# Differential attention beside slab matmuls: logits of two steps behind every second slab, their weights' transposes in the middle of a later one

## Chip, cores and metric

One core of one Trainium2 chip. The time is the device time of one launch in microseconds; several runs are taken and their median is compared.

## The reference

Two blocks of two layers each on 512 tokens of width 1024. The stage in question belongs to the first block (`first_block`), once in each of its two layers: four heads of differential attention, whose scores come in two maps of width 64.

```python
scores = jnp.einsum('bqhmd,bkhmd->bhmqk', qb, kh)
p = jax.nn.softmax(jnp.where(mask, scores, -jnp.inf), axis=-1)
w = p[:, :, 0] - lam * p[:, :, 1]
return jnp.einsum('bhqk,bkhd->bqhd', w, vf)
...
merged = (g[:, :, 0] * (y_a @ w_branch_a[layer])
          + g[:, :, 1] * (y_b @ w_branch_b[layer])
          + g[:, :, 2] * (y_c @ w_branch_c[layer]))
```

## The kernel before

**Slabs.** Every dense product runs as slabs of 128 x 1024 weights in three terms of fp32r (high x high, high x low, low x high; lines 576 to 578), 24 matmuls of 512 columns for a slab of eight tiles (`slab_t`, line 585). A slab is loaded by SP into one of four raw buffers as soon as the slab four before it is done (`load`, line 547), its high part made by ACT (`split_hi`, line 562, called as `hi_ahead` for the slab three on) and its low part by DVE in place (`split_lo`, called as `lo_ahead` for the slab three on, line 571). All engines run in program order, so a wait holds whatever stands behind it.

**The fill stage.** Attention of the first block is spread over 19 slabs (`FILLS1`, `for n in range(FILLS1)` on PE at line 2251, ACT at 1018, DVE at 1572): slabs 0 to 4 are gates of branch b, 5 to 12 branch b's product (`w_branch_b`), 13 to 18 gates of branch c. Sixteen steps (four heads h by four query tiles qi) go with them. Step n has logits for two maps of (qi + 1) x 128 columns, each map in 64 rows of the array (line 2276), so that the two run beside each other.

- PE: slab n with its `between(k)` ahead of tile k; behind the slab the logits of step n, then the transposes of the weights of step n - 2 (`LAG`), qi + 1 of them (line 657). `by_v` of head h (line 2231) stands ahead of tile 3 of slab 4h + 6 (`PV1_AT`) and first waits until the four steps' transposes have been copied out.
- DVE at step n: causal mask, maximum and its negative for both maps (lines 1580 to 1582); in slabs 0 to 3 two casts of `yb` to its high part (line 1588), whose low part POOL then makes (line 560); from slab 5 on the merge of branch b (lines 1595 and 1599); then, once both exponentials have left their banks, the weights of step n (lines 1606 to 1610); last `lo_ahead` of slab n.
- ACT at step n: `hi_ahead` of slab n; the copy of `by_v`'s result (line 1023); copies of gates (line 957); the copies of the transposed weights of step n - 2 (line 1048); the exponentials of step n (line 1057).

**PSUM.** `pm` has four banks, used in turn in the order in which the schedule `PM` hands out numbers: `take_pm` (line 639) makes PE wait until use i - 4 has been left (`pm_free`). Logits take two uses a step, transposes and `by_v` one each. The order of `PM.take` calls (lines 348 to 357) must be that of PE's program.

**Other buffers.** Exponentials and weights of step n lie in `ee[n % 3]`; the exponentials of step n wait for the transposes of step n - 3.

Of the kernel before, what the change touches and what calls it, by code (L numbers as in the profile page):

```python
# [10 lines left out]
ACT = mybir.ActivationFunctionType  # L11
# [102 lines left out]
def program(nc, t, out, depth=DEPTH, depth2=DEPTH):  # L114
    with ExitStack() as ctx:
# [231 lines left out]
        SUMS_AT = FILLS1 - 2  # L347
        for n in range(FILLS1):
            if n in PV1_AT:
                PM.take(("pv", PV1_AT.index(n)), 1)  # L350
            if n == SUMS_AT:
                PM.take("sub_first", 1)
            if n < STEPS:
                PM.take(("score", n), 2)
            if LAG <= n < STEPS + LAG:
                PM.take(("w_t", n - LAG), 1)
# [459 lines left out]
        def _(act):  # L816
# [48 lines left out]
            for l in range(depth):  # L865
# [152 lines left out]
                for n in range(FILLS1):  # L1018
# [8 lines left out]
                    if n == SUMS_AT:  # L1027
                        u = PM["sub_first"]
                        nc.scalar.activation(sub_sum[:, 0:DA_H - 1, :].rearrange("p h t -> p (h t)"), sums_of(pm_filled(act, u), TT * (DA_H - 1)), ACT.Copy)\
                            .then_inc(pm_free[u % 4], 1)  # L1030
                    if n < GATES_B_IN:
                        gates(gate, SL["gate_b"], UN["gate_b"], KD - GATES_B_IN + n, 1, ACT.Copy)
# [8 lines left out]
                    if LAG <= n < STEPS + LAG:  # L1041
                        k = n - LAG
                        h, qi, u = k // TT, k % TT, PM[("w_t", k)]
                        if h >= 2:
                            act.wait_ge(pm_ready, PM[("pv", h - 2)] + 1)
                        bank = pm_filled(act, u)
                        for kt in range(qi + 1):
                            done = nc.scalar.activation(wt(h, kt)[:, (qi - kt) * P:(qi - kt + 1) * P], bank[:, kt * P:(kt + 1) * P], ACT.Copy)
                        done.then_inc(pm_free[u % 4], 1)
                    if n < STEPS:  # L1050
                        qi = n % TT
                        if n >= 3:
                            act.wait_ge(pm_ready, PM[("w_t", n - 3)] + 1)
                        for m in range(2):
                            u, o = PM[("score", n)] + m, 8 * n + 2 * m
                            act.wait_ge(S("neg_max"), past("neg_max") + 2 * n + m + 1)
                            nc.scalar.activation(ee[n % 3][:, m, 0:(qi + 1) * P], pmb(u)[:, 0:(qi + 1) * P], ACT.Exp,
                                                 bias=sst[:, o + 1:o + 2], scale=DA_D ** -0.5,
                                                 accum_out=sst[:, 8 * n + 4 + m:8 * n + 5 + m]).then_inc(pm_free[u % 4], 1)
# [259 lines left out]
        def _(dve):  # L1319
# [44 lines left out]
            for l in range(depth):  # L1364
# [207 lines left out]
                for n in range(FILLS1):  # L1572

                    if n < STEPS:
                        qi = n % TT
# [1108 lines left out]
```

## Time and profile before

| | us |
|---|---|
| median of three runs | 2553.91 (2553.7 to 2556.19) |
| the profiled execution, its time | 2558.13 |
| the profiled execution, its span | 2556.4 |
| PE busy in the span | 2535.5 |
| DVE busy | 1598.4 |
| ACT busy | 1171.6 |
| POOL busy | 323.0 |

The fill stage of the first layer lies at about 364 to 500 us, that of the second at about 1290 to 1431. In the rows a matmul counts from its start; matmuls overlap, so the distance between two starts, not the duration, is what one costs. An fp32 product shows as two matmul instructions.

### The profile page before, as it was taken

Reading aid. Unit: us, or ns where it says so; the run is one execution under the profiler, and the core shown is the slowest. Engines: PE = TensorE matmul, PEld = TensorE weight load, DVE = VectorE, ACT = ScalarE, POOL = GpSimd, SP = SyncE. Lnnn points to the kernel's source line nnn. Section 1 sums busy time; section 2 is a strip of 40 time slices with the busy share of each in tenths; the row PEclk is TensorE's granted clock in tenths of the full one; section 3 lists DMA queues with packets and bytes.
Section 4 is the critical chain, followed back from the end, with each engine's and each line's share of the span. In section 5 each row is a group of like instructions: output and inputs, shape, how many; then the busy total and the mean of one; then the engine's idle time right before and its main releaser. Section 6 shows DMA issues by size and latency. Waiting matters only on the chain.

```text
span 2556.4 us, 34401 instructions
## 1 busy us (share of the span) xinstructions
PE 2535.5 (99%) x12345; PEld 2059.7 (81%) x12345; DVE 1598.4 (63%) x2484; ACT 1171.6 (46%) x2124; POOL 323.0 (13%) x256
## 2 busy tenths in 40 slices
PE   8999999999999999999999999999999999999998
PEld 7887887788888887887877888888888777887777
DVE  6745767567777336637667457775345677647765
ACT  6434544434433235436353444333246555575463
POOL 1024200010111001225010201110010001110010
PEclk9999999999999999999999999999999999999999
DMA  5543342333333455442443333333324322332322
GB/s 128 104 83 66 85 90 75 62 103 91 98 98 92 100 104 89 91 79 71 92 82 64 82 95 93 96 98 93 100 79 107 83 65 61 87 95 75 83 61 72
DMA packets 417919, 221.93 MB, mean 87 GB/s; under 512 B 52705, under 2 KB 400897, under 8 KB 417537
## 3 DMA queue, kind: packets, MB, share of 16 engines
q1 hardware_dynamic: 417792, 220.26, 35.5%
q8 instruction: 78, 1.28, 0.2%
q14 instruction: 49, 0.39, 0.1%
HBM read 218.12 MB, written 2.10 MB: 86 GB/s over the span
## 4 chain that ended last, share of the span: by engine, by line
PE 93%; DVE 2%; DMA 2%; ACT 1%; issue 1%; POOL 0%; SPq 0%; ACTq 0%; DVEq 0%
PE pg L576 28%; PE pg L578 27%; PE pg L577 27%; PE pm L657 3%; DMA w_raw<-in_w_in_dram 1%; PE pm L2395 1%; DVE w_lo L571 1%; PE pm L2276 1%; PE pm L2369 1%; PE pm L2231 1%; PE pm L2179 1%; PE pm L2409 1%; PE pm L2436 1%; ACT w_hi L566 0%; PE pm L2182 0%
## 5 line engine op out<-in xcount | busy, mean ns | idle before, releaser
L571 DVE TENSOR_TENSOR w_lo<-w_raw,w_hi 128x1024 fp32r<-128x1024 f32 (+3 forms) x440 | 535.4, 1218 | 485.0 <-ACT w_hi L566 482.9
L576 PE MATMUL pg<-h_hi,w_hi 128*128 128x512 f32 x1856 | 738.0, 398 | 1.1 <-DVE conv_in L1804 0.8
L566 ACT ACTIVATE w_hi<-w_raw 128x1024 fp32r<-128x1024 f32 (+3 forms) x440 | 434.7, 988 | 641.4 <-DMA w_raw<-in_w_in_dram 279.1
L578 PE MATMUL pg<-h_hi,w_lo 128*128 128x512 f32 x1856 | 723.9, 390 | 0.0
L577 PE MATMUL pg<-h_lo,w_hi 128*128 128x512 f32 x1856 | 723.5, 390 | 0.0
L576 PEld LDWEIGHTS pg<-h_hi,w_hi 128*128 128x128 f32 x1856 | 349.3, 188 | 74.6 <-issue 6.0
L578 PEld LDWEIGHTS pg<-h_hi,w_lo 128*128 128x128 f32 x1856 | 348.7, 188 | 74.2
L577 PEld LDWEIGHTS pg<-h_lo,w_hi 128*128 128x128 f32 x1856 | 349.3, 188 | 68.7 <-issue 1.0
L576 PE MATMUL pg<-w_hi,h_hi 128*128 128x512 f32 (+2 forms) x448 | 167.3, 373 | 0.6 <-issue 0.6
L578 PE MATMUL pg<-w_hi,h_lo 128*128 128x512 f32 (+2 forms) x448 | 165.1, 369 | 0.0
L577 PE MATMUL pg<-w_lo,h_hi 128*128 128x512 f32 (+2 forms) x448 | 165.0, 368 | 0.0
L1669 DVE SCALAR_TENSOR_TENSOR arena<-conv_in,par,arena 128x512 f32<-128x512 f32 x176 | 131.8, 749 | 15.2 <-DVE arena L1669 10.6
L576 PE MATMUL pg<-f_hi,w_hi 128*128 128x512 f32 x352 | 138.7, 394 | 0.0
L578 PE MATMUL pg<-f_hi,w_lo 128*128 128x512 f32 x352 | 138.0, 392 | 0.0
L577 PE MATMUL pg<-f_lo,w_hi 128*128 128x512 f32 x352 | 136.6, 388 | 0.0
L1105 ACT ACTIVATE arena<-conv_in,par 128x512 f32<-128x512 f32 x88 | 71.9, 817 | 114.3 <-DVE conv_in L1663 114.3
L560 POOL TENSOR_TENSOR f_lo<-arena,f_hi x44 | 56.8, 1291 | 519.8 <-DVE f_hi L1677 519.8
L1663 DVE TENSOR_TENSOR conv_in<-pg,rinv 128x512 f32<-128x512 f32 x88 | 60.8, 691 | 88.7 <-PE pg L578 79.7
L576 PE MATMUL pg<-nb_parts,w_hi 128*128 128x512 f32 x256 | 102.5, 401 | 0.0
L578 PE MATMUL pg<-nb_parts,w_lo 128*128 128x512 f32 x256 | 100.6, 393 | 0.0
L576 PEld LDWEIGHTS pg<-w_hi,h_hi 128*128 128x128 f32 x448 | 84.4, 188 | 13.9 <-issue 1.9
L578 PEld LDWEIGHTS pg<-w_hi,h_lo 128*128 128x128 f32 x448 | 84.3, 188 | 12.9
(405 smaller groups left out, 3765.2 us busy)
## 6 DMA issues: line engine op xcount, KB each, us to landing
w_raw<-in_w_in_dram SPq DMA_DIRECT2D x184, 512.0 KB, 5.0
w_raw<-in_ffn_w_up_dram SPq DMA_DIRECT2D x88, 512.0 KB, 3.8
w_raw<-in_w_out_dram SPq DMA_DIRECT2D x32, 512.0 KB, 3.9
w_raw<-in_ffn_w_down_dram SPq DMA_DIRECT2D x32, 512.0 KB, 3.8
w_raw<-in_w_branch_b_dram SPq DMA_DIRECT2D x16, 512.0 KB, 3.8
w_raw<-in_ffn_w_down_dram SPq DMA_DIRECT2D x16, 384.0 KB, 3.4
w_raw<-in_w_branch_a_dram SPq DMA_DIRECT2D x16, 256.0 KB, 2.8
w_raw<-in_w_branch_c_dram SPq DMA_DIRECT2D x16, 256.0 KB, 2.8
```

The costliest lines, as they stand in the source:

```text
L560: return nc.gpsimd.tensor_tensor(lo, value, hi.bitcast(F32), ALU.subtract)
L566: nc.scalar.activation(w_hi[:, s % HI, 0:n], w_raw[:, s % RAW, 0:n], ACT.Copy).then_inc(hi_done, 1)
L571: nc.vector.tensor_tensor(w_lo[:, s % RAW, 0:n], w_raw[:, s % RAW, 0:n], w_hi[:, s % HI, 0:n].bitcast(F32), ALU.subtract)\
L576: nc.tensor.matmul(dst, l_hi, r_hi, start=start, stop=False)
L577: nc.tensor.matmul(dst, l_hi, r_lo, start=False, stop=False)
L578: return nc.tensor.matmul(dst, l_lo, r_hi, start=False, stop=stop)
L657: done = nc.tensor.transpose(dst, src, ident[0:src.shape[0], 0:src.shape[0]])
L1105: nc.scalar.activation(facc[:, j, :], conv_in[:, j, 4:4 + SEQ], ACT.Identity, bias=fconv_b[:, bass.ds(i, 1)], scale=fconv_w[:, i, 2:3]).th ...
L1663: nc.vector.tensor_tensor(conv_in[:, j, 4:4 + SEQ], unit_filled(dve, SL["up"] + j, UN["up"] + j, 4, it), inv[:, :], ALU.mult)\
L1669: nc.vector.scalar_tensor_tensor(facc[:, j, :], conv_in[:, j, 4 - a:4 - a + SEQ], fconv_w[:, i, 2 - a:3 - a], facc[:, j, :], ALU.mult, ALU ...
L2179: done = nc.tensor.matmul(bank[rows, c * P:(c + 1) * P], xdt[:, c, h * 64:h * 64 + 64], seg[:, h % 4, c, :], start=True, stop=c == 0)
L2231: done = nc.tensor.matmul(bank[:, kt * P:SEQ], qkv[:, kt, 1024 + h * P:1024 + (h + 1) * P], wt(h, kt), start=kt == 0, stop=kt == TT - 1)
```

## The change

Logits of steps n and n + 1 follow each other behind slab n for even n (`SCORES_AT`), none behind odd slabs. The transposes of both steps stand together ahead of tile 4 of slab n + 2 (`W_AT`), no longer behind a slab. ACT and DVE take two steps at even n and none at odd n; ACT's copies of the transposed weights now stand ahead of the gates' copies. The numbers in `PM` follow the new order.

```diff
--- before.py
+++ after.py
@@ -345,15 +345,18 @@
         GATES_C_IN = FILLS1 - KD - GATES_B_IN
         PV1_AT = [TT * (h + 1) + LAG for h in range(DA_H)]
         SUMS_AT = FILLS1 - 2
+        SCORES_AT, W_AT = range(0, STEPS, 2), range(2, STEPS + 1, 2)
         for n in range(FILLS1):
             if n in PV1_AT:
                 PM.take(("pv", PV1_AT.index(n)), 1)
+            if n in W_AT:
+                PM.take(("w_t", n - 2), 1)
+                PM.take(("w_t", n - 1), 1)
             if n == SUMS_AT:
                 PM.take("sub_first", 1)
-            if n < STEPS:
+            if n in SCORES_AT:
                 PM.take(("score", n), 2)
-            if LAG <= n < STEPS + LAG:
-                PM.take(("w_t", n - LAG), 1)
+                PM.take(("score", n + 1), 2)
         PM.take("sub_last", 1)
         PM.take("sub_spread", DA_H)
         for name in ("sums2", "spread2"):
@@ -1028,6 +1031,14 @@
                         u = PM["sub_first"]
                         nc.scalar.activation(sub_sum[:, 0:DA_H - 1, :].rearrange("p h t -> p (h t)"), sums_of(pm_filled(act, u), TT * (DA_H - 1)), ACT.Copy)\
                             .then_inc(pm_free[u % 4], 1)
+                    for k in (n - 2, n - 1) if n in W_AT else ():
+                        h, qi, u = k // TT, k % TT, PM[("w_t", k)]
+                        if h >= 2:
+                            act.wait_ge(pm_ready, PM[("pv", h - 2)] + 1)
+                        bank = pm_filled(act, u)
+                        for kt in range(qi + 1):
+                            done = nc.scalar.activation(wt(h, kt)[:, (qi - kt) * P:(qi - kt + 1) * P], bank[:, kt * P:(kt + 1) * P], ACT.Copy)
+                        done.then_inc(pm_free[u % 4], 1)
                     if n < GATES_B_IN:
                         gates(gate, SL["gate_b"], UN["gate_b"], KD - GATES_B_IN + n, 1, ACT.Copy)
                     if n == GATES_B_IN:
@@ -1038,25 +1049,16 @@
                     if i >= 0:
                         act.wait_ge(S("b_merged"), past("b_merged") + i + 1)
                         gates(gate, SL["gate_c"], UN["gate_c"], i, 1, ACT.Copy)
-                    if LAG <= n < STEPS + LAG:
-                        k = n - LAG
-                        h, qi, u = k // TT, k % TT, PM[("w_t", k)]
-                        if h >= 2:
-                            act.wait_ge(pm_ready, PM[("pv", h - 2)] + 1)
-                        bank = pm_filled(act, u)
-                        for kt in range(qi + 1):
-                            done = nc.scalar.activation(wt(h, kt)[:, (qi - kt) * P:(qi - kt + 1) * P], bank[:, kt * P:(kt + 1) * P], ACT.Copy)
-                        done.then_inc(pm_free[u % 4], 1)
-                    if n < STEPS:
-                        qi = n % TT
-                        if n >= 3:
-                            act.wait_ge(pm_ready, PM[("w_t", n - 3)] + 1)
+                    for k in (n, n + 1) if n in SCORES_AT else ():
+                        qi = k % TT
+                        if k >= 3:
+                            act.wait_ge(pm_ready, PM[("w_t", k - 3)] + 1)
                         for m in range(2):
-                            u, o = PM[("score", n)] + m, 8 * n + 2 * m
-                            act.wait_ge(S("neg_max"), past("neg_max") + 2 * n + m + 1)
-                            nc.scalar.activation(ee[n % 3][:, m, 0:(qi + 1) * P], pmb(u)[:, 0:(qi + 1) * P], ACT.Exp,
+                            u, o = PM[("score", k)] + m, 8 * k + 2 * m
+                            act.wait_ge(S("neg_max"), past("neg_max") + 2 * k + m + 1)
+                            nc.scalar.activation(ee[k % 3][:, m, 0:(qi + 1) * P], pmb(u)[:, 0:(qi + 1) * P], ACT.Exp,
                                                  bias=sst[:, o + 1:o + 2], scale=DA_D ** -0.5,
-                                                 accum_out=sst[:, 8 * n + 4 + m:8 * n + 5 + m]).then_inc(pm_free[u % 4], 1)
+                                                 accum_out=sst[:, 8 * k + 4 + m:8 * k + 5 + m]).then_inc(pm_free[u % 4], 1)
 
                     if n == STEPS - 1:
                         act.wait_ge(slab_done, SL["b"] + KD)
@@ -1571,10 +1573,10 @@
                 chain(nc.vector.scalar_tensor_tensor(lstat[:, 4:5], lstat[:, 3:4], lam_c[:, 0:1], lstat[:, 2:3], ALU.subtract, ALU.subtract))
                 for n in range(FILLS1):
 
-                    if n < STEPS:
-                        qi = n % TT
+                    for k in (n, n + 1) if n in SCORES_AT else ():
+                        qi = k % TT
                         for m in range(2):
-                            u, o = PM[("score", n)] + m, 8 * n + 2 * m
+                            u, o = PM[("score", k)] + m, 8 * k + 2 * m
                             bank = pm_filled(dve, u)
                             diag = bank[:, qi * P:(qi + 1) * P]
                             chain(nc.vector.tensor_tensor(diag, diag, causal, ALU.add))
@@ -1598,14 +1600,14 @@
                         unit_left(dve, UN["a"] + i)
                         nc.vector.tensor_tensor(m_val[:, i, :], m_val[:, i, :], gate[:, i, :], ALU.add).then_inc(S("b_merged"), 1)
 
-                    if n < STEPS:
-                        w = (n % TT + 1) * P
+                    for k in (n, n + 1) if n in SCORES_AT else ():
+                        w = (k % TT + 1) * P
                         for m in range(2):
-                            pm_left(dve, PM[("score", n)] + m)
-                        o = 8 * n + 4
+                            pm_left(dve, PM[("score", k)] + m)
+                        o = 8 * k + 4
                         chain(nc.vector.reciprocal(sst[:, o + 2:o + 4], sst[:, o:o + 2]))
                         chain(nc.vector.tensor_scalar(sst[:, o + 3:o + 4], sst[:, o + 3:o + 4], lstat[:, 4:5], None, ALU.mult))
-                        e0, e1 = (ee[n % 3][:, m, 0:w] for m in range(2))
+                        e0, e1 = (ee[k % 3][:, m, 0:w] for m in range(2))
                         chain(nc.vector.tensor_scalar(e0, e0, sst[:, o + 2:o + 3], None, ALU.mult))
                         nc.vector.scalar_tensor_tensor(e0, e1, sst[:, o + 3:o + 4], e0, ALU.mult, ALU.add).then_inc(S("w_ready"), 1)
                     lo_ahead(FILL0() + n, 0, 0)
@@ -2258,6 +2260,11 @@
                             heads_t(k // 2)
                         if n in PV1_AT and k == 3:
                             by_v(PV1_AT.index(n))
+                        if n in W_AT and k == 4:
+                            for step in (n - 2, n - 1):
+                                pe.wait_ge(S("w_ready"), past("w_ready") + step + 1)
+                                transposes(pe, PM[("w_t", step)], lambda bank: [(bank[:, kt * P:(kt + 1) * P], ee[step % 3][:, 0, kt * P:(kt + 1) * P])
+                                                                                for kt in range(step % TT + 1)])
                         if n == SUMS_AT and k == 5:
                             sub_sums(PM["sub_first"], range(DA_H - 1))
                         if n == FILLS1 - 1 and k == 7:
@@ -2266,20 +2273,15 @@
                     i = n - GATES_B_IN
                     of_b = 0 <= i < KD
                     slab_t(pe, FILL0() + n, UN["b"] + i, 0, 0, yb_hi if of_b else hh, h_parts(yb_lo) if of_b else hl, KD, ready=between)
-                    if n < STEPS:
-                        h, qi = n // TT, n % TT
+                    for step in (n, n + 1) if n in SCORES_AT else ():
+                        h, qi = step // TT, step % TT
                         for m in range(2):
                             if qi == 0:
                                 pm_left(pe, PM["qk_t"] + 2 * h + m)
                         for m in range(2):
                             r = slice(DA_D * m, DA_D * m + DA_D)
-                            nc.tensor.matmul(take_pm(pe, PM[("score", n)] + m)[:, 0:(qi + 1) * P], q_t[r, h, qi * P:(qi + 1) * P],
+                            nc.tensor.matmul(take_pm(pe, PM[("score", step)] + m)[:, 0:(qi + 1) * P], q_t[r, h, qi * P:(qi + 1) * P],
                                              k_t[r, h, 0:(qi + 1) * P], start=True, stop=True).then_inc(pm_ready, 1)
-                    if LAG <= n < STEPS + LAG:
-                        k = n - LAG
-                        pe.wait_ge(S("w_ready"), past("w_ready") + k + 1)
-                        transposes(pe, PM[("w_t", k)], lambda bank: [(bank[:, kt * P:(kt + 1) * P], ee[k % 3][:, 0, kt * P:(kt + 1) * P])
-                                                                     for kt in range(k % TT + 1)])
                 for i in range(GATES_C_IN, KD):
                     def between(k):
                         h = KD * (i - GATES_C_IN) + k - 6
```

## Rows read from the trace of the kernel before

**Rows 1.** The page, busy time of the matmuls and its share of the span.

```profile
PE 2535.5 (99%) x12345; PEld 2059.7 (81%) x12345; DVE 1598.4 (63%) x2484; ACT 1171.6 (46%) x2124; POOL 323.0 (13%) x256
```

**Rows 2.** Waits of PE, 365 to 1430: total us, times, longest.

```profile
PE pm L2231 <- ACT conv_in L1048: 2.3, 2, 1.4
PE pm L2231 <- ACT rinv L1048: 1.9, 1, 1.9
```

**Rows 3.** Timeline of PE around step 0's logits (start us, us, engine, line).

```profile
369.68 0.40 PE L577 MATMUL pg<-h_lo,w_hi 128*128 128x512 f32 x1
369.92 0.40 PE L578 MATMUL pg<-h_hi,w_lo 128*128 128x512 f32 x1
370.24 0.49 PE L2276 MATMUL pm<-arena 64*128 64x128 f32 x4
370.66 0.50 PE L576 MATMUL pg<-h_hi,w_hi 128*128 128x512 f32 x1
371.00 0.40 PE L577 MATMUL pg<-h_lo,w_hi 128*128 128x512 f32 x1
```

**Rows 4.** Windows: stretch, length, PE, PEld, DVE, ACT, POOL, clock, DMA, GB/s.

```profile
376.03:376.98 0.95, 0.95 (x6) 0.30 (x4) 0.91 (x2) 0.45 (x1) 0.95 (x1) 1.00 0.02 4
402.21:403.58 1.37, 1.37 (x10) 0.71 (x9) 1.03 (x2) 1.36 (x2) 0.00 (x0) 1.00 0.00 0
482.59:483.07 0.48, 0.48 (x6) 0.38 (x4) 0.00 (x0) 0.48 (x3) 0.00 (x0) 1.00 0.02 7
463.54:465.85 2.31, 2.31 (x11) 1.46 (x9) 1.86 (x5) 0.24 (x2) 0.00 (x0) 1.00 1.01 70
1421.87:1426.31 4.44, 2.55 (x11) 1.39 (x9) 1.92 (x2) 2.65 (x8) 0.00 (x0) 1.00 0.08 23
```

**Rows 5.** Windows over DVE's parts of single steps, columns as above.

```profile
372.66:374.11 1.45, 1.45 (x8) 1.21 (x7) 1.31 (x6) 0.91 (x3) 0.00 (x0) 1.00 0.74 171
378.45:380.16 1.71, 1.71 (x9) 1.39 (x8) 1.57 (x8) 0.56 (x2) 0.00 (x0) 1.00 0.74 217
374.86:377.32 2.46, 2.46 (x13) 1.54 (x12) 2.35 (x6) 0.79 (x1) 2.38 (x2) 1.00 0.10 31
408.27:409.51 1.24, 1.24 (x7) 1.02 (x7) 1.13 (x4) 1.24 (x2) 0.00 (x0) 1.00 0.02 7
443.58:444.91 1.33, 1.33 (x8) 1.08 (x7) 1.30 (x3) 0.67 (x2) 0.00 (x0) 1.00 0.28 86
412.71:417.46 4.75, 4.75 (x22) 3.91 (x23) 4.47 (x12) 2.68 (x6) 0.00 (x0) 1.00 0.39 114
419.54:424.76 5.22, 5.22 (x24) 4.31 (x25) 4.94 (x12) 2.95 (x7) 0.00 (x0) 1.00 0.37 100
```

**Rows 6.** Timeline of DVE, second pass over step 0's weights.

```profile
376.13 1.26 DVE L1610 SCALAR_TENSOR_TENSOR arena<-arena,rinv 128x128 f32<-128x128 f32 x1
```

**Rows 7.** Timeline of POOL beside it.

```profile
374.61 2.64 POOL L560 TENSOR_TENSOR yb_lo<-arena,nb_parts 128x512 fp32r<-128x512 f32 x2 [97.57 <-DVE nb_parts L1588]
```

**Rows 8.** Timeline of ACT, slabs 13 to 15; in brackets idle, releaser.

```profile
462.10 0.77 ACT L1048 ACTIVATE conv_in<-pm 128x128 f32<-128x128 f32 x4
...
469.72 1.06 ACT L566 ACTIVATE w_hi<-w_raw 128x1024 fp32r<-128x1024 f32 x1 [5.93 <-DMA w_raw<-in_w_in_dram]
470.68 0.58 ACT L1023 ACTIVATE arena<-pm 128x512 f32<-128x512 f32 x1
...
1410.89 1.06 ACT L566 ACTIVATE w_hi<-w_raw 128x1024 fp32r<-128x1024 f32 x1 [9.50 <-DMA w_raw<-in_w_in_dram]
```

**Rows 9.** Windows, from a slab's mark to ACT's next waiting split.

```profile
446.93:452.76 5.83, 5.83 (x27) 3.99 (x26) 4.73 (x12) 3.06 (x8) 0.00 (x0) 1.00 0.46 95
460.23:469.72 9.49, 9.49 (x44) 6.75 (x44) 4.02 (x11) 3.12 (x11) 0.00 (x0) 1.00 0.70 56
1387.35:1396.03 8.68, 7.81 (x36) 5.31 (x35) 4.11 (x12) 3.13 (x11) 0.00 (x0) 1.00 0.48 68
1397.36:1410.89 13.53, 13.53 (x61) 9.77 (x60) 6.68 (x17) 2.43 (x7) 0.00 (x0) 1.00 0.53 57
```

## The prediction

> **What bounds it.** I read the page first: PE is busy 99% of the span [rows 1], so a change counts by what it adds to or takes from PE's queue. The granted clock is 1.00, the 2.4 GHz level, in every stretch of [rows 4, 5], so I leave it out. Then I asked the waits of PE alone over both layers' fill stages. Only the product with the values, `by_v`, waits for long there: 2.3 us in two waits and 1.9 in one, each for ACT's copy of a transposed weight [rows 2]. Last, the starts of PE's instructions give each insertion's price: matmuls of a slab start 0.24 to 0.23 us apart [rows 3], so from the last of a slab to the first of the next is 0.23 with nothing between, and what exceeds that is the insertion. I count from the start of a slab's last matmul ("the mark"); the windows of [rows 4] reach from the mark to the next slab's first matmul.
>
> **The switches saved.** Step 0's logits alone make the gap 0.74 us [rows 3], step 1's 0.95 [rows 4]: a further 128 columns cost 0.21. So 0.74 - 0.23 - 0.21 = 0.30, and 0.11 by which the slab's second matmul comes later than its spacing (0.34 behind the first [rows 3]), don't depend on the width: 0.4 an insertion. Of it 0.09 lie ahead of the first 64-row matmul (0.32 after the mark instead of 0.23), 0.11 behind the insertion, the rest between its halves. A second step put right behind the first saves the first two parts, 0.2; the gaps between halves stay. The bounds are 0 and 0.4 for each of 8 pairs in 2 layers: 0 to 6.4 us. I take 3.2, because the halves of one step show the gap between them as well.
> The transposes lose a little. Three of them alone make a gap of 0.48 [rows 4], 0.25 over the plain one and about 0.35 with the late matmul behind, 0.12 each; four behind logits add 1.37 - 0.95 = 0.42 [rows 4], 0.1 each. I take 0.05 a step lost, 1.4 us over the 28 steps that stand behind logits now. Net: **1.8 us less**; the bounds are +1.4 and -5.
> The Trainium skill (TensorEngine Tiling (Array Packing), Key Properties) says that a change of tiling mode drains TensorE. That agrees with the 0.32 against the plain 0.23 of [rows 3] and speaks for pairing the logits. By it alone no figure comes out; the sum doesn't use it.
>
> **The waits that go.** `by_v` of head h sits in slab 4h+6, ahead of its fourth tile. Now it waits for the copies of step 4h+3, transposed only behind slab 4h+5, some 2 us before. After the change that step is transposed in slab 4h+4, over a slab and a half earlier. Its copies stand behind one ACT split that waits for a load, and still have some 9 us. A `by_v` without a wait takes 2.31 from mark to slab matmul, the longest waiting one 4.44 [rows 4], so a wait of 1.9 costs 0.24 more to restart. Three waits are 4.2 [rows 2] and 0.7: **4.9 us less** (the lower bound of the gain is 0, if another wait takes their place).
>
> **New wait 1: weights in slab 2.** Steps 0 and 1 must be normalized by slab 2's fifth tile. DVE starts the maxima at 372.66, 2.74 after slab 0's mark at 369.92 [rows 3], late because of a weight split. Then maxima of steps 0 and 1 are 1.45 + 1.71, two casts 0.75, weights of step 0 2.46, of step 1 1.24 [rows 5]: ready at 380.3. PE: the pair's gap is 0.23 + 0.51 + 0.72 less 0.09 = 1.37, slab 1 from first start to mark 5.37 (370.66 [rows 3] to 376.03 [rows 4]), 12 matmuls of slab 2 (2.75) and one transpose, with the plain gaps, come to 379.7. Wait 0.6, restart 0.1, in both layers: **1.4 us more** (0 to 4).
> The 2.46 is what the trace has while POOL splits: step 0's second pass over 128 columns takes 1.26 [rows 6] and ends just behind POOL's pair of operations, 374.61 + 2.64 [rows 7]; all of step 1's passes, twice as wide, take less than that together. Step 1's 1.24 is from a place with POOL idle.
> That row weighs against a cheap rule. The Trainium skill (SBUF — State Buffer, "Who interferes with whom") has the DVE–GpSimd pair as an exclusive lock for a whole instruction. With it the 2.46 stays; without it step 0 would need about 1.2 less and there would be no wait. It also speaks against the change at DVE's splits L571, which now follow the casts at once; there the loser would stand about 1.3 longer.
> Slab 4 needs steps 2 and 3. In general, step 2's and step 3's chains are 4.75 + 5.22 with a 1.33 merge in each [rows 5]; one merge counts once per pair, so 8.64, plus an estimated 0.95 from the logits' start to DVE's first read (two halves at the widths' slope): 9.6. PE arrives 10.5 after that start: the rest of the pair's gap (2.2 by the same slope, less the 0.32 ahead of it), a slab 5.37, a plain gap, half a slab 2.75, three transposes 0.3. That leaves 0.9. At slab 4 the casts (0.75) stand for the merge, but POOL adds 1.3: nothing left, and I price it at 0 to 1 each, taken 0.
>
> **New wait 2: a PSUM bank behind ACT.** `pm` has four banks, taken in the order of `PM`. After the change slab 14 ends with logits 14 and 15 in the banks last held by logits 13, `by_v` of head 2, and the transposes of 12 and 13. ACT must copy those out first, and its copies stand behind the split of the slab three on, which waits for that slab's load. In the trace this split starts 9.49 us after slab 13's mark in the first layer and 8.68 in the second [rows 9], held by DMA [rows 8]. The value copy starts 0.96 later and takes 0.58 [rows 8]: free at 11.08 and 10.27. PE would be at the second half of step 14 after 0.23 + 5.23 (23 spacings) + 2.17 (`by_v`: 2.31 - 0.23 and the 0.09 to 0.11 behind it) + 0.35 + 0.32 = 8.3. Wait **2.75 + 1.95 = 4.7 us**.
> At slab 12 there are seven transposes and no `by_v`. ACT's split starts 5.83 after slab 11's mark [rows 9]; seven copies follow at 0.96 and need 0.77 for four [rows 8] and 0.16 for each further, 1.25: 8.1. PE is at step 13's logits at 0.23 + 5.27 + 0.78 + 0.32 + 0.43 = 7.05. Wait 1.05, taken for both layers: **2.1 us**. Slabs 4 and 8 load from `w_branch_b` sooner, as no ACT split there is held long; slabs 6 and 10 have three copies only. Slab 16 has no logits behind it.
> What is queued behind ACT's wait: the copies of the gates and the exponentials; behind DVE's: the merge and the low part of slab n+3, which has its cover of a whole slab. Nothing else waits. The bounds of this term: 0, if loads land within 6.5 us of the mark, and 13.6 for slab 14 alone, if both take the 13.53 of the second layer's slab 15 [rows 9].
>
> **Moved, at no cost.** The same DVE, ACT and DMA instructions run; SP's queue is untouched, its loads follow the slabs' ends. The exponentials of an odd step now run ahead of ACT's next split, which frees DVE sooner.
>
> **Sum.** -1.8 - 4.9 + 1.4 + 4.7 + 2.1 = **+1.5 us**. Against the profiled execution's 2558.13 us (span 2556.4 and 1.7 around it) that is 2559.6; that execution is 4.2 above the median of the three runs, 2553.91, so I forecast 2555.4. What a measurement can tell from no change is 0.2%, 5.1 us.
>
> **Rivals.**
> - *Loads late, slower.* The bank waits decide all: if the loads behind slabs 12 and 14 land 2 to 3 us later than read, four waits grow by that, +9 to +13. It decides from about 1 us. For it: the same weights' loads vary from 5.83 to 13.53 [rows 9]. Against: at slab 14 both layers agree within 0.8. Net +6 to +14, 2568 at the most. Chance 0.17.
> - *DVE late in every even slab, slower.* The 0.9 of slack is eaten at slabs 8, 12 and 16 by semaphore delays or by exponentials that come late, and slab 4 waits 1: six waits of 0.5 to 1, net +4 to +8, 2560. By the skill's lock rule on L571 slabs 2 and 4 would be the places. The casts of slabs 1 and 3 come while DVE has more than 2 us to spare, so against it. Chance 0.10.
> - *Banks free in time, faster.* If ACT isn't held at 12 and 14, the sum is -6.7 + 1.4 = -5.3, 2548.6; with the full 0.4 a pair -8.5, 2545.4. For it: `by_v`'s waits are certain to go. Against: [rows 8]. Chance 0.18.
> - *Nothing moves:* the waits of `by_v` only change their place. Chance 0.03.
> - My forecast, -3 to +6 about the median: chance 0.52.
>
> **Numbers.** A quarter of the fast rival and most of my forecast are within 0.2%. Faster 0.17 (the fast rival's 0.14 and a tail), same 0.58, slower 0.25 (0.15 of the late loads, 0.05 of DVE, 0.05 my forecast's tail). Range 2548 to 2562: it takes in the fast rival's near half and late loads up to +8, and leaves out the rest.
>
> **What would show it.** In the profile after: no wait at `by_v`'s line; gaps from mark to slab matmul of 1.4 for the logits of steps 0 and 1 and 2.2 for 2 and 3; the transposes in the fifth tile of every even slab; waits of PE's logits for ACT's copies at slabs 14 (2 to 3 us) and 12 (about 1); a short wait of the transposes for DVE at slab 2. It would be wrong if the logits never wait (then faster), or if transposes wait for DVE at slabs 8, 12, 16 (then slower).

## The result, and the profile after

| | before, us | after, us |
|---|---|---|
| median of 14 runs each | 2555.14 (2553.52 to 2556.97) | 2558.96 (2557.12 to 2561.76) |
| ratio, 95% interval | | 1.0016 [1.0009, 1.0023] |
| the profiled execution, its time | 2558.13 | 2558.61 |
| its span | 2556.4 | 2556.9 |

The change costs 3.8 us. That lies in the forecast's range and within the 0.2% called the same. The two profiled executions differ by only 0.5 us, because that of before is 3.0 above its own median: how much of a stall one execution shows will matter below.

The page of the kernel after, against [rows 1]: the weight loads (PEld) are busy 5.0 us longer, though PE isn't busier; nothing else moved by more than 2 us.

```profile
PE 2534.8 (99%) x12345; PEld 2064.7 (81%) x12345; DVE 1598.3 (63%) x2484; ACT 1172.2 (46%) x2124; POOL 325.0 (13%) x256
```

So I compare stretches. The first view gives the windows from slab 0's mark to slab 18's last matmul, both layers, first of the kernel after, then of the kernel before in a second profiled execution of it (unchanged, taken among the experiments). Columns as in [rows 4].

```profile
369.66:504.05 134.39, 131.39 (x602) 100.04 (x601) 88.76 (x205) 61.36 (x147) 12.69 (x8) 0.99 0.32 70
1299.34:1431.40 132.06, 129.78 (x602) 99.38 (x601) 88.85 (x205) 60.54 (x147) 12.69 (x8) 1.00 0.36 72
```

```profile
370.17:500.62 130.45, 130.36 (x602) 97.47 (x601) 89.57 (x205) 61.23 (x147) 10.92 (x8) 1.00 0.32 72
1296.37:1428.44 132.07, 130.62 (x602) 97.40 (x601) 88.62 (x205) 61.23 (x147) 10.91 (x8) 1.00 0.36 72
```

I call the sum of the two lengths **the stage**: 266.45 after, 262.52 before; 3.9 us, about the whole difference of the medians. And the first layer's window after has a clock of 0.99, not 1.00. The profile of before that the prediction read has a stage of 265.45:

```profile
369.92:500.37 130.45, 130.38 (x603) 97.47 (x602) 89.57 (x205) 61.22 (x147) 10.92 (x8) 1.00 0.32 72
1295.72:1430.72 135.00, 130.85 (x603) 97.24 (x601) 87.73 (x205) 60.23 (x147) 10.85 (x8) 1.00 0.35 70
```

Waits of PE over both stages, kernel after. Against [rows 2], `by_v` (now L2233) is gone; the logits (L2283) now wait for ACT's copies of `by_v`'s result and of transposed weights, the transposes (L660) for DVE's weights.

```profile
PE pm L2283 <- ACT arena L1026: 3.0, 2, 1.9
PE pm L660 <- DVE arena L1612: 1.5, 2, 0.7
PE pm L2283 <- ACT conv_in L1040: 0.7, 2, 0.3
```

Windows of the kernel after, from the start of the last slab matmul ahead of an insertion to the next slab matmul, to be read against [rows 4]. In order: the logits behind slab 4 (as wide as those of steps 0 and 1), behind slab 6 (as wide as 2 and 3), the transposes in slab 2 and in slab 4, the logits behind slab 12 in either layer, and behind slab 14 in either layer.

```profile
396.85:398.03 1.18, 1.18 (x11) 0.53 (x9) 1.17 (x2) 0.76 (x2) 1.18 (x1) 1.00 0.00 0
411.42:413.45 2.03, 2.03 (x11) 0.70 (x9) 0.73 (x2) 0.00 (x0) 0.00 (x0) 1.00 0.19 48
378.92:380.35 1.43, 0.70 (x6) 0.34 (x4) 1.32 (x5) 0.00 (x0) 0.00 (x0) 1.00 0.74 222
393.04:394.23 1.19, 1.14 (x10) 0.81 (x8) 1.19 (x2) 0.00 (x0) 0.00 (x0) 1.00 0.79 237
453.35:455.82 2.47, 2.12 (x11) 0.90 (x9) 1.49 (x7) 2.27 (x11) 0.00 (x0) 1.00 0.16 31
1383.02:1385.47 2.45, 2.12 (x10) 0.89 (x8) 1.46 (x7) 2.25 (x11) 0.00 (x0) 1.00 0.15 32
469.15:474.99 5.84, 3.97 (x10) 1.32 (x8) 2.50 (x8) 3.57 (x10) 0.00 (x0) 0.82 0.30 59
1398.81:1402.90 4.09, 2.93 (x11) 1.13 (x9) 1.73 (x5) 3.09 (x8) 0.00 (x0) 1.00 0.34 34
```

The pairs' gaps without a wait are 1.18 and 2.03; forecast were 1.4 and 2.2. Without a wait the transposes take 0.48 in slab 2 and 0.92 in slab 4 (in E3's trace below).

Slab 14 in the first layer stands out: 5.84 against 4.09, at a clock of 0.82. Timelines of that place, ACT's and then PE's (against [rows 8]):

```profile
470.66 1.06 ACT L569 ACTIVATE w_hi<-w_raw 128x1024 fp32r<-128x1024 f32 x1 [8.41 <-DMA w_raw<-in_w_in_dram]
471.62 0.58 ACT L1026 ACTIVATE arena<-pm 128x512 f32<-128x512 f32 x1
```

```profile
469.47 0.91 PE L2283 MATMUL pm<-arena 64*128 64x384 f32 x2
472.25 2.81 PE L2283 MATMUL pm<-arena 64*128 64x384 f32 x6 [1.87 <-ACT arena L1026]
474.99 0.79 PE L579 MATMUL pg<-h_hi,w_hi 128*128 128x512 f32 x1
```

This is the wait that was forecast: the split idles for its load, the copy of `by_v`'s result behind it frees the bank at 472.2, and only then does PE start the second map of step 14. What was not forecast follows: those six instructions take 2.74 us to the next slab matmul, where the second layer's take 1.70 (1401.20 to 1402.90). The windows behind show why:

```profile
472.25:473.00 0.75, 0.75 (x3) 0.69 (x5) 0.00 (x0) 0.75 (x4) 0.00 (x0) 0.90 0.18 57
473.00:474.00 1.00, 1.00 (x4) 0.33 (x1) 0.57 (x2) 0.75 (x3) 0.00 (x0) 0.50 0.25 59
474.00:475.00 1.00, 1.00 (x4) 0.01 (x1) 0.93 (x4) 0.49 (x2) 0.00 (x0) 0.50 0.34 67
475.00:476.00 1.00, 1.00 (x3) 0.82 (x3) 0.93 (x4) 0.49 (x3) 0.00 (x0) 0.50 0.18 55
476.00:477.00 1.00, 1.00 (x5) 0.85 (x4) 0.93 (x4) 0.71 (x3) 0.00 (x0) 0.87 0.17 55
```

The granted clock is at 0.50, the 1.2 GHz level, after 1.87 us in which PE stood still. I call such a stretch a **spell** of half clock. What the five rows withhold is 0.75 x 0.10 + 3 x 0.50 + 0.13 = **1.7 us**. The trace of before had this price too, at a place that the prediction didn't look at, long ahead of the stage:

```profile
42.00:43.00 1.00, 0.00 (x0) 0.00 (x0) 0.42 (x1) 1.00 (x2) 1.00 (x1) 1.00 0.05 0
43.00:44.00 1.00, 0.72 (x3) 0.31 (x4) 1.00 (x2) 1.00 (x3) 0.23 (x1) 0.84 0.05 0
44.00:45.00 1.00, 1.00 (x4) 0.67 (x3) 1.00 (x2) 0.98 (x2) 0.02 (x1) 0.50 0.15 34
```

PE waits 2.4 us (no matmul from 42 to 43), starts again, and the clock falls behind it; with the next three windows of 0.50, 0.50 and 0.95 that is again 1.7 us. That wait is in all 14 profiled executions of this case, the spell behind it in 12 (E9 and the second run of E3, below, keep a clock of 1.00 there).

Last, DVE ahead of slab 2's transposes and just behind, and POOL beside it, to be read against [rows 6, 7]:

```profile
376.67 0.87 DVE L1611 TENSOR_SCALAR arena<-arena,rinv 128x128 f32<-128x128 f32 x1
377.58 1.28 DVE L1612 SCALAR_TENSOR_TENSOR arena<-arena,rinv 128x128 f32<-128x128 f32 x1
...
379.62 0.48 DVE L1612 SCALAR_TENSOR_TENSOR arena<-arena,rinv 128x256 f32<-128x256 f32 x1
380.02 1.22 DVE L574 TENSOR_TENSOR w_lo<-w_raw,w_hi 128x1024 fp32r<-128x1024 f32 x1
...
381.82 2.32 DVE L574 TENSOR_TENSOR w_lo<-w_raw,w_hi 128x1024 fp32r<-128x1024 f32 x1
```

```profile
376.06 2.66 POOL L563 TENSOR_TENSOR yb_lo<-arena,nb_parts 128x512 fp32r<-128x512 f32 x2 [99.27 <-DVE nb_parts L1590]
381.65 3.62 POOL L563 TENSOR_TENSOR yb_lo<-arena,nb_parts 128x512 fp32r<-128x512 f32 x2 [2.94 <-DVE nb_parts L1590]
```

Step 0's passes are long only while POOL works; the pass over twice the width, once POOL is done, takes 0.48. Step 1's weights are ready at 380.1, 10.4 us after slab 0's mark at 369.66; forecast was 380.3 with the mark at 369.92, the same 10.4.

### The profile page after: what moved, and what is told of

Read it like the earlier page. It is cut to its first block, busy times and chain, and to the rows that moved or that the text cites. A ratio compares the mean times of both kernels' runs of the same rounds, so it can differ in the third digit from the quotient of the medians.

```text
span 2556.9 us, 34401 instructions
## 1 busy us (share of the span) xinstructions
PE 2534.8 (99%) x12345; PEld 2064.7 (81%) x12345; DVE 1598.3 (63%) x2484; ACT 1172.2 (46%) x2124; POOL 325.0 (13%) x256
## 3 DMA queue, kind: packets, MB, share of 16 engines
q8 instruction: 78, 1.28, 0.2%
## 4 chain that ended last, share of the span: by engine, by line
PE 93%; DVE 3%; issue 1%; DMA 1%; ACT 1%; POOL 0%; SPq 0%; ACTq 0%; DVEq 0%
PE pg L579 28%; PE pg L581 27%; PE pg L580 27%; PE pm L660 3%; PE pm L2397 1%; PE pm L2283 1%; DMA w_raw<-in_w_in_dram 1%; DVE w_lo L574 1%; PE pm L2371 1%; PE pm L2181 1%; PE pm L2233 1%; PE pm L2411 1%; PE pm L2438 1%; ACT w_hi L569 0%; PE pm L2184 0%
## 5 line engine op out<-in xcount | busy, mean ns | idle before, releaser
L574 DVE TENSOR_TENSOR w_lo<-w_raw,w_hi 128x1024 fp32r<-128x1024 f32 (+3 forms) x440 | 539.6, 1228 | 499.7 <-ACT w_hi L569 497.8
```

Source lines behind the costliest of these rows:

```text
L574: nc.vector.tensor_tensor(w_lo[:, s % RAW, 0:n], w_raw[:, s % RAW, 0:n], w_hi[:, s % HI, 0:n].bitcast(F32), ALU.subtract)\
```

## The experiments

Each block of results gives medians of runs beside runs of before on the same chip. "Stage" is the sum defined above.

**The kernels as they are, once more.** Three executions of the change and two of before are profiled in all.

> The changed kernel once more, for its waits in a second profile. My theory of the result: logits behind ACT's copies wait at slabs 14 (4.05 and 2.05 us in the first profile) and 12 (1.3 each), transposes wait for DVE in slabs 2 (0.95 each) and 4 (0.27 each). Expected again: no wait at by_v, the slab 14 waits between 1.5 and 5 (they follow the load's landing), the others within 0.2. Rival, that the slab 14 waits are an accident of one execution: gone or below 0.5 here. Time 1.0016 of before, as measured.

Measured: 2559.61 (10 runs) to 2555.31, ratio 1.0017 [1.0008, 1.0027]; stage 267.01. The excess of each gap over the same gap without a wait is 0.95 a layer at slab 2, 0.27 at slab 4, 1.28 and 1.83 at slab 12 (1.29 and 1.27 in the first profile, so one of them missed the 0.2 that was allowed), 2.75 and 1.95 at slab 14. But the half clock is at another place, behind slab 12's wait in the second layer, where PE had stood idle 0.90 us. Slab 14's wait in the first layer has 1.85 us idle again, and the clock stays at 1.00 from 471 to 480.

```profile
1382.22:1385.24 3.02, 2.12 (x11) 0.90 (x9) 1.93 (x8) 2.91 (x12) 0.00 (x0) 1.00 0.25 46
...
1386.00:1387.00 1.00, 1.00 (x4) 0.78 (x3) 0.96 (x3) 0.77 (x4) 0.00 (x0) 0.54 0.77 121
1387.00:1388.00 1.00, 1.00 (x4) 0.81 (x3) 0.93 (x4) 0.07 (x1) 0.00 (x0) 0.50 0.42 63
```

> The kernel before once more, for a second profile. My theory: the first one, 3 us above the median, had more waits of by_v (4.2 us in three) than most executions; here they come to 1 to 4 us with the time moving along, the gaps without waits equal to within 0.02 us each. Rival: the waits are the same 4.2 again, and the difference between profile and median lies elsewhere.

Measured: one time, 2555.72, and a stage of 262.52. `by_v` waits less than in [rows 2], where three waits made 4.2:

```profile
PE pm L2231 <- ACT conv_in L1048: 1.4, 2, 1.0
```

**E1: ACT's copies ahead of its split**, in slabs with transposes. It takes away what holds the bank, not the wait's instruction.

```diff
-                    hi_ahead(FILL0() + n)
+                    if n not in W_AT:
+                        hi_ahead(FILL0() + n)
...
                         done.then_inc(pm_free[u % 4], 1)
+                    if n in W_AT:
+                        hi_ahead(FILL0() + n)
```

> In even slabs 2 to 16 ACT takes by_v's copy and the transposes' copies ahead of its split for the slab three on, so that no copy stands behind a load. My theory (the logits of slabs 12 and 14 wait for banks that ACT frees behind that split): these waits, 8.7 us in the profile, go; about 2550.5, 0.998 of before, 8 us under the changed kernel. Rival 1 (PE waits there for something else, the load itself or DVE): no change against the changed kernel, 2559. Rival 2 (the split, now later, makes the slab's low part late): a new wait of slab matmuls for DVE, 2555 or more.

Measured: 2550.15 (11 runs), ratio 0.998 [0.9971, 0.9989], 9.5 less than the change beside it; stage 257.55. The only wait of PE in it is that for DVE; slab 14's logits take what those of slab 6 take, at full clock:

```profile
PE pm L660 <- DVE arena L1615: 1.5, 2, 0.7
```

```profile
468.28:470.30 2.02, 2.02 (x10) 0.69 (x8) 0.72 (x2) 0.50 (x1) 0.00 (x0) 1.00 0.40 66
```

The order on ACT is what the change lost by. The forecast's rival "banks free in time" had put this case at 5.3 under before; 5.2 are measured, with the same errors in it that cancel (below).

**E2: DVE's casts of `yb` last**, so that POOL works when the weights are done.

```diff
-                    if n == 0:
-                        dve.wait_ge(pm_ready, PM["qk_t"] + 8)
-                    if n < 4:
-                        for i in (2 * n, 2 * n + 1):
-                            nc.vector.tensor_copy(yb_hi(i), yb[:, i, :]).then_inc(S("yb_hi_done"), 1)
...
                     lo_ahead(FILL0() + n, 0, 0)
+                    if n == 0:
...
```

> In slabs 0 to 3 DVE's casts, which start POOL, come behind the weights and the low part instead of ahead of them; nothing else. My theory (the weights of steps 0 and 1 are late at slab 2 because POOL's splits hold DVE's two passes): the waits of slab 2 (0.95 each) and 4 (0.27 each) go, 2.4 us in both layers, 2556.5. Rival (DVE is late by its own amount of work, started late at slab 0): only the casts' own 0.75 is saved ahead of the weights, so 0.2 to 0.3 stays at slab 2, gain 1.5 at most; against both: if by the late casts branch b's low parts are late at slab 5, a new wait there of 1 us or more.

Measured: 2557.65 (10 runs), ratio 1.0007 [0.9998, 1.0017], 2.0 less than the change beside it; stage 266.29. The same two passes of DVE, with POOL idle:

```profile
376.35 0.29 DVE L1606 TENSOR_SCALAR arena<-arena,rinv 128x128 f32<-128x128 f32 x1
376.67 0.35 DVE L1607 SCALAR_TENSOR_TENSOR arena<-arena,rinv 128x128 f32<-128x128 f32 x1
```

The waits of slabs 2 and 4 are gone (2.4 us). The two passes are 1.51 us shorter, which alone is more than slab 2's 0.95; the casts' own 0.75 wouldn't be. In the profiled execution about 1.8 came back as bank waits that the change hadn't: logits at slab 2 and 10 of the second layer 0.68 and 0.86 late, at slab 4 of the first 0.27. A likely reason, not tested: PE reaches these places sooner, and the loads that hold ACT there don't come sooner by as much. But this execution, 2559.21, is the slowest of the ten, 1.6 above their median. The stage's 0.2 us of gain is that of one execution; the medians' 2.0, near the 2.4 expected, is the better measure. The half clock is there too, behind slab 14.

**E3: both remedies.**

> Both edits. If the two kinds of wait are independent, their gains add: 8.7 + 2.4 = 11 us under the changed kernel, about 2548, 0.997 of before. Rival (the waits hide one another, since a wait gives DVE time for the next): 2550 or more, and new waits of transposes for DVE at slabs 8, 12 or 16.

Measured: 2547.51 (6 runs), ratio 0.9968 [0.9956, 0.998]. Its stage is 127.52 and 127.53. It was run a second time beside the kernels of the last block:

> The kernel with both remedies once more, beside the other three: 2547.5 us, stage of 136.3 us in both layers with no wait and no spell of half clock in it.

Measured: 2548.04 (9 runs), ratio 0.9972 [0.9962, 0.9981], no wait and no spell, and 127.52 us in both layers (the expected 136.3 must count a longer stretch, since this one took 127.52 in the first run already; which one isn't on record):

```profile
369.92:497.44 127.52, 127.52 (x602) 98.65 (x601) 87.76 (x205) 62.14 (x147) 12.55 (x8) 1.00 0.33 74
```

PE is busy all of it. This is the change without its waits, 11.4 us less of stage than the change, and **faster than both kernels**, 7.4 to 7.8 under before (0.3%).

**E7: before with `by_v` late**, four tiles later in its slab except in the last, so that it waits for nothing.

```diff
-                        if n in PV1_AT and k == 3:
+                        if n in PV1_AT and k == (3 if n == FILLS1 - 1 else 7):
```

> The kernel before with by_v ahead of tile 7 instead of tile 3 in slabs 6, 10 and 14: its copies get 2.7 us more, everything else is as before. My theory (those waits cost 1 to 3 us in a typical run): 2553 to 2554.3, 0.9992 to 0.9996 of before, no wait at by_v but that of slab 18. Rival (the change's loss in the median came because there was little to gain here): same as before within 0.3 us.

Measured: 2553.47 (11 runs), ratio 0.9995 [0.9986, 1.0004], 2.0 less than before, though the interval holds no change; stage 260.28, no wait:

```profile
370.09:500.22 130.13, 130.13 (x602) 97.56 (x601) 89.60 (x205) 61.64 (x147) 10.94 (x8) 1.00 0.32 72
1295.97:1426.12 130.15, 130.15 (x602) 97.53 (x601) 89.22 (x205) 61.29 (x147) 10.89 (x8) 1.00 0.36 73
```

The eleven executions fall in two groups, six at 2552.9 to 2553.5 and five at 2554.5 to 2555.6; the profiled one is of the first, and four of the five list a mean clock of 0.998 where the first lists 0.999 or 1.00. What the slower ones had isn't profiled.

So `by_v`'s waits were 5.2 us in the profile that the prediction read and 2.2 in the second. E3's 255.04 against this 260.28 is the change's new order with all waits out on both sides: **5.2 us less**.

**E5 and E4: the parts of the new order.** E5 moves each step's transposes from behind slab n + 2 to ahead of its tile 4 and leaves the logits single, with both remedies; E4 is E5 with the logits in pairs.

The diffs: E5 against before, then E4 against E5; the numbers in `PM`, ACT's copies and DVE's steps follow the order.

```diff
+                        if LAG <= n < STEPS + LAG and k == 4:
+                            step = n - LAG
+                            pe.wait_ge(S("w_ready"), past("w_ready") + step + 1)
...
-                    if LAG <= n < STEPS + LAG:
-                        k = n - LAG
```

```diff
-                    if n < STEPS:
-                        h, qi = n // TT, n % TT
+                    for step in (n, n + 1) if n in SCORES_AT else ():
+                        h, qi = step // TT, step % TT
```

> Logits of one step behind each slab, as before, the transposes of one step ahead of tile 4 of every slab; the copies ahead of ACT's split and the casts last, as in the best kernel, so that nothing should wait. My theory (the pairing of the logits is what saves in PE's queue, 0.4 us a pair; parting transposes from logits costs 0.05 a step): by_v's waits gone (2.6 us in a typical run), 1.6 us added, about 2554.3, 0.9996 of before. Rival (the middle of the slab is what is good, one change of kind less): as fast as the best kernel, 2547.5.

> As the run before it, but logits of two steps behind every second slab. It differs from it in the pairing of logits alone. My theory: 16 pairs at 0.4 us less, 6.4 us under it, about 2548, within 0.5 us of the best kernel. Rival (0.2 a pair, as I had predicted): 3.2 us under it, 2551.

Measured: E5 2556.79 (11 runs), ratio 1.0004 [0.9995, 1.0013], stage 263.98; E4 2548.29 (7 runs), ratio 0.9971 [0.996, 0.9983], stage 255.52, no wait. E5 is 2.5 above what was expected; 1.6 of that is a wait of its own in one layer, for step 15's weights:

```profile
PE pm L657 <- DVE arena L1608: 1.4, 1, 1.4
```

Without it E5's stage is twice its first layer's 131.17, 262.34. First layers of E5 and of E4:

```profile
369.93:501.10 131.17, 131.17 (x602) 97.60 (x601) 84.84 (x205) 62.48 (x147) 10.59 (x8) 1.00 0.31 72
369.88:497.64 127.76, 127.76 (x602) 98.18 (x601) 87.74 (x205) 62.17 (x147) 12.54 (x8) 1.00 0.33 74
```

So the pairing of logits is worth 262.34 - 255.52 = 6.82, or **0.43 for each of 16 pairs**. The gaps say nearly the same: E5's logits of steps 2 and 3 alone, and E4's of both.

```profile
382.51:383.68 1.17, 1.17 (x7) 0.31 (x5) 0.78 (x3) 0.60 (x1) 0.65 (x1) 1.00 0.00 0
389.32:390.70 1.38, 1.38 (x7) 0.31 (x5) 0.67 (x2) 0.60 (x1) 0.97 (x1) 1.00 0.00 0
```

```profile
382.01:384.03 2.02, 2.02 (x10) 0.69 (x8) 2.02 (x4) 0.70 (x2) 1.66 (x2) 1.00 0.12 30
```

1.17 + 1.38 less one plain 0.23 is 2.32, against 2.02: 0.30, and the 0.11 by which a slab's second matmul comes late is paid once less. Taking the transposes away from the logits costs 262.34 - 260.28 = 2.1 (E7's `by_v` at tile 7 takes the same 2.31 as at tile 3), and putting two steps of them together gives 0.5 back (255.52 to 255.04).

**E8 and E9: is the half clock part of the price?** E8 is E3 with the old order on ACT in slab 14 alone: one wait a layer, nothing else. E9 is the change with the copies first in slab 14 alone: the other waits, without this one. The diffs: E8 against E3, then E9 against the change.

```diff
-                    if n not in W_AT:
+                    if n not in W_AT or n == 14:
                         hi_ahead(FILL0() + n)
...
-                    if n in W_AT:
+                    if n in W_AT and n != 14:
                         hi_ahead(FILL0() + n)
```

```diff
-                    hi_ahead(FILL0() + n)
+                    if n != 14:
+                        hi_ahead(FILL0() + n)
...
+                    if n == 14:
+                        hi_ahead(FILL0() + n)
```

> The kernel with both remedies, but in slab 14 alone ACT splits before it copies, as in the change. So one wait a layer is put back, 2.6 and 2.05 us in the change's profile, 2.75 and 1.95 in its repeat. Theory A (the price of a wait is its idle time): 4.7 more than with both remedies, 2552.2 us, granted clock 1.00 all through the stage. Theory B (a wait of this length can also bring the half clock behind it, which cost 1.7 in one spot of each profiled execution of the change): one such spell in the profile within 4 us behind slab 14's logits in at least one layer, stage and median 6.4 to 8 above both remedies, 2554 to 2555.6.

Measured: 2554.6 (11 runs), ratio 0.9998 [0.9989, 1.0007], 6.6 above E3 beside it; stage 261.46, 6.4 above. The windows over slab 14's logits in either layer and one behind the first:

```profile
467.13:472.97 5.84, 3.99 (x10) 1.35 (x8) 2.50 (x8) 3.57 (x10) 0.00 (x0) 0.81 0.29 58
...
472.00:473.00 1.00, 1.00 (x4) 0.03 (x1) 0.93 (x4) 0.51 (x2) 0.00 (x0) 0.50 0.33 66
...
1394.57:1398.59 4.02, 2.93 (x11) 1.14 (x9) 1.73 (x5) 3.09 (x8) 0.00 (x0) 1.00 0.29 33
```

The second layer pays 4.02 - 2.02 = 2.0 for its wait; the first layer's length is 131.93 - 127.52 = 4.4 over E3's, of which 1.7 is withheld clock and 2.7 the wait. 4.7 + 1.7 is the 6.4: theory B, at the low end of what it gave; A's 4.7 is 1.9 short of the medians' difference, and E8's eleven executions lie within 1.5 us. Nine of them list a mean clock of 0.998, none of E3's nine beside it does: the spell isn't the profiled execution's alone.

> The change with ACT's copies of the transposed weights ahead of its split in slab 14 alone; slab 12's bank wait (1.3 to 1.8 a layer) and slab 2's and 4's waits for DVE stay. Theory A (waits alone): 4.7 below the change, 2554.3. Theory B (the half clock comes behind slab 14's wait): 4.7 and 1.7 below, 2552.6, and no spell of half clock in the stage. Theory C (any of the waits in a row brings it, since the repeat of the change had it behind slab 12): a spell behind slab 12, 2554.3.

Measured: 2553.22 (11 runs), ratio 0.9992 [0.9983, 1.0001]; stage 260.61, no clock below 1.00 in it, slab 12's waits still there and one of 0.16 at slab 8:

```profile
1378.18:1381.07 2.89, 2.12 (x10) 0.89 (x8) 1.86 (x8) 2.89 (x12) 0.00 (x0) 1.00 0.26 49
```

B's 2552.6 is 0.6 away and A's and C's 2554.3 is 1.1; the interval, some 2 us to either side, holds both. The profile is B's. But the repeat of the change had its spell behind slab 12, so C isn't excluded for other executions.

> The change once more, for its clock. Theory B: one spell of about 3.4 us at the half clock in the stage, behind slab 12's or slab 14's wait, as in both profiled executions so far; theory A has no reason for one and takes the two for chance. Time 2557 to 2562 either way.

Measured: one time, 2560.25, stage 266.80, with one spell of half clock behind slab 14 in the first layer.

Taken together: slab 14's wait is in five profiled executions (three of the change, E2, E8), and each has exactly one spell of 1.7 us in the stage; nine without it (two of before, E1, E3 twice, E4, E5, E7, E9) have none. What makes one wait bring the spell and another not stays open. The length of the wait alone doesn't: slab 14's 1.85 to 1.87 us idle in the first layer brought it four times of five, its 1.06 to 1.18 in the second never, slab 12's 0.90 once. And "one a run" is shown for profiled executions only. Of the change's 24 timed ones, two list a mean clock of 1.00, at 2557.5 us, so they had probably no spell in the stage; four of E7's, without slab 14's wait, list the 0.998 that goes with one.

## Why the prediction came out as it did

The total was off by 3.6 us, 2555.4 against 2558.96. Of that, 1.2 is the base: the median of the three runs shown was 2553.91, that of all 14 is 2555.14. The other 2.3 are the terms, in us for both layers:

| term | forecast | runs |
|---|---|---|
| new order without waits (E3 to E7) | -1.8 | -5.2 |
| `by_v`'s waits go | -4.9 | -2.2 (5.2 in the profile read) |
| slab 2 waits for DVE | +1.4 | +1.9 |
| slab 4 waits for DVE | 0 | +0.5 |
| slab 12 waits for a bank | +2.1 | +2.6 to 3.1 |
| slab 14 waits for a bank | +4.7 | +4.7 |
| half clock behind a wait | none | +1.7 |
| sum | +1.5 | +4.0 to 4.5; medians +3.8 |

The prediction's sums for the banks are off by a few hundredths: 9.49 + 0.96 + 0.58 is 11.03, not 11.08, and the second layer's is 10.22, so its own numbers give 4.65 at slab 14 and 2.0 at slab 12.

**What held.** The waits came where they were put: `by_v`'s went, slab 14 has the largest, with 4.7 forecast and 4.7 measured, and it is ACT's split that holds the bank (E1). Slab 2 waits because DVE stands beside POOL (E2), and no transposes wait at slabs 8, 12 and 16, so that rival fell. The rival "loads late" didn't come either: the length of slab 14's wait agreed within 0.15 in all executions.

**The step that failed: "The granted clock is 1.00, the 2.4 GHz level, in every stretch of [rows 4, 5], so I leave it out."** Only one of these stretches holds a wait of PE, `by_v`'s 1.9 us, which was followed by no fall of the clock. From that one case the text left the clock out for a kernel to which it gave four more waits, of 1 to 2.8 us, and it didn't look at the fall at 43 us in the same trace. The change's own waits brought the clock down, 1.7 us in each of its three profiled executions and in E8. The Trainium skill (TensorE: Matmul & The Clock Gate, Part 1) says that the clock is set by how busy the engine has been of late; this case's traces agree in so far as every spell in the stage stands behind a wait. The same Part 1 of the Trainium skill also says that the point at which the clock rises varies from run to run. Here the fall varies too: behind slab 14 in two executions of the change, behind slab 12 in the third.

**The pair, mis-sized.** "I take 3.2" of 0 to 6.4 was the middle of two bounds. The runs show 6.8, just above the upper one: all that didn't depend on the width was saved, the gap between halves as well. The argument for the middle was that the halves of one step show such a gap too; the runs show that only one of the two steps pays it. On the other side the transposes cost 2.1 by being moved, against 1.4 forecast, and 0.5 of it came back by pairing them.

**`by_v`, right for one execution.** 4.9 was forecast and 5.2 were in that profile. But its time stood 4.2 over the median of the runs shown, and 3.0 of that were just these waits; the sum took them at full size and then put the result against the median. Taken at 2.2, the forecast would have been 2558.

**The small waits.** Slab 2 was 0.25 a layer short. DVE was ready when forecast (10.4 us after the mark); PE came earlier, 0.2 of it by the pair's gap, 1.18 instead of 1.37. Slab 4 was put at 0 from a slack of "nothing left", with 0 to 1 as its bounds: 0.27 a layer. The lock that the prediction weighed by [rows 6, 7] also caught DVE's split L574, 2.32 instead of 1.22 us, and stretched POOL's pair from 2.66 to 3.62. Forecast was that the loser stands about 1.3 longer; it was 1.1. That the lock speaks against the change there was right of the mechanism; PE paid 0.27 a layer at most, at slab 4.

Two errors of 3.4 and 2.7 on the gain's side nearly cancelled, which is luck; the clock and the waits that were longer than forecast, 3.2 to 3.7 us, are what was left. The sign of the sum was right, by less merit than its size suggests.

## What to carry to other kernels

Before rotating banks are shared anew, follow the engine that empties them through its program order: a copy that stands behind an instruction waiting for a load holds the bank, and moving it ahead cost nothing here (-9.5 us, and the change turned from a loss into a gain by that alone). A new wait of TensorE of 1 to 2 us is to be priced with a possible fall of the clock behind it, by a spell that the trace shows elsewhere; the spell can come or stay away, so it belongs in the range at least. And a stall that one execution shows is read from two before it goes into a sum, above all where that execution is far from the median.

## What the runs showed of the hardware

- TensorE's clock fell to the 1.2 GHz level after it had stood for 1.85 to 1.87 us (the change twice, E2, E8) and once for 0.90 (the change's repeat), had started again and run at the full clock for 0.6 to 2.1 us; each spell cost 1.7 us. The same 1.85 in the repeat, `by_v`'s 1.9 in [rows 2] and slab 14's 1.16 in the second layer were followed by none, and a wait of 2.4 at 42 us by one in 12 of 14 executions. So whether a wait of this size brings a spell can differ between two executions of one kernel.
- A DVE operation on two SBUF operands beside POOL's took 2.32 instead of 1.22 us, and POOL's pair 3.62 instead of 2.66: both sides pay. That agrees with the Trainium skill (SBUF — State Buffer, "Who interferes with whom"), which calls it an exclusive lock for a whole instruction.
- Pairs of half-array logits pay what they cost beyond streaming once for the pair: 0.4 us saved at either width (a gap of 1.18 for 128 and 256 columns, of 2.03 for 384 and 512).
